# gMLP mixing on column halves of the array, a 768-byte gap between FFN operands, and an alternating unit order

## What is computed

```python
u, v = split(gelu(h @ w_in)); v = rms_norm(v, v_gain)           # both [T, 1024]
ws = where(chunk_causal_mask(128), w_s, 0.0)                    # 16 groups of [128, 128]
vb = v.reshape(B, nb, 128, 16, 64)                              # blocks of 128 rows, groups of 64 channels
mixed = einsum('gpq,bnqgd->bnpgd', ws, vb) + b_s                # mixing of rows inside a block, by group
out = (u * mixed) @ w_out
```

## Time and profile before

| | |
|---|---|
| median of 3 runs | 2557.38 us (2556.01 to 2557.67) |
| profiled execution, own time | 2556.86 us |
| its span, first to last instruction | 2555.1 us |
| TensorE (PE) busy | 2500.5 us, 98% of the span, 16343 matmuls |
| weight loads (PEld) busy | 2424.3 us, 95% |
| VectorE (DVE), ScalarE (ACT), GpSimd (POOL) busy | 1513.9, 890.7, 258.8 us |
| large products on `gx` / on `h` | 10368 / 3168 matmuls of 128x352 |
| mixing matmuls, L1867 | 288 instructions, 33.9 us busy |
| mean granted TensorE clock | 0.991 |

### The profile page before, as it was taken

The page is one execution under the profiler, slowest core; times in us unless marked ns, Lnnn a source line. Parts: engine busy times, 40 slices in busy tenths (PEclk is TensorE's granted clock), DMA queues, the critical chain, the costliest instruction groups (busy, mean ns, idle before and its releaser), DMA issues.

```text
span 2555.1 us, 42749 instructions
## 1 busy us (share of the span) xinstructions
PE 2500.5 (98%) x16343; PEld 2424.3 (95%) x16343; DVE 1513.9 (59%) x2833; ACT 890.7 (35%) x1663; POOL 258.8 (10%) x569
## 2 busy tenths in 40 slices
PE   7999999999999999999999999999999999999998
PEld 7888888889899999999999999999999999999998
DVE  4555555567766666666666524334666666666666
ACT  5444444445422222222234531234222333222223
POOL 0111111102100000000001420221000000000003
PEclk9999999999999999999999999999999999999999
DMA  5222222444111011111111210111111111110112
GB/s 145 69 59 59 59 59 59 138 117 141 50 50 49 33 44 38 42 40 49 49 49 34 68 33 17 51 50 50 34 50 49 49 49 49 49 49 33 38 45 78
DMA packets 136980, 145.29 MB, mean 57 GB/s; under 512 B 4940, under 2 KB 126452, under 8 KB 136884
## 3 DMA queue, kind: packets, MB, share of 16 engines
q1 hardware_dynamic: 121844, 118.82, 14.6%
q0 software_dynamic: 14384, 23.03, 3.4%
q10 hardware_dynamic: 656, 2.12, 0.2%
HBM read 125.97 MB, written 17.97 MB: 56 GB/s over the span
## 4 chain that ended last, share of the span: by engine, by line
PE 89%; DVE 5%; ACT 3%; POOL 2%; issue 1%; DMA 0%; ACTq 0%; DVEq 0%; POOLq 0%
PE psum L158 26%; PE psum L160 26%; PE psum L159 26%; PE psum L1003 2%; PE psum L1024 2%; PE psum L986 2%; POOL total L229 1%; PE psum L1867 1%; DVE gx_lo L217 1%; PE psum L901 0%; ACT conv_t L1545 0%; DVE w_lo L763 0%; DVE conv_t L1615 0%; DVE conv_t L1618 0%; ACT w_hi L759 0%
## 5 line engine op out<-in xcount | busy, mean ns | idle before, releaser
L158 PE MATMUL psum<-gx_hi,w_hi 128*128 128x352 f32 x3456 | 1131.2, 327 | 15.7 <-DVE gx_lo L217 6.7
L159 PE MATMUL psum<-gx_lo,w_hi 128*128 128x352 f32 x3456 | 1119.5, 324 | 0.0
L160 PE MATMUL psum<-gx_hi,w_lo 128*128 128x352 f32 x3456 | 1118.6, 324 | 0.0
L158 PEld LDWEIGHTS psum<-gx_hi,w_hi 128*128 128x128 f32 x3456 | 652.7, 189 | 20.7 <-issue 14.3
L159 PEld LDWEIGHTS psum<-gx_lo,w_hi 128*128 128x128 f32 x3456 | 653.2, 189 | 0.6 <-issue 0.5
L160 PEld LDWEIGHTS psum<-gx_hi,w_lo 128*128 128x128 f32 x3456 | 652.9, 189 | 0.0
L1642 DVE TENSOR_TENSOR x<-x,psum 128x352 f32<-128x352 f32 x528 | 259.3, 518 | 123.0 <-PE psum L160 123.0
L1545 ACT ACTIVATE conv_t<-a_gate,cur 128x352 f32<-128x352 f32 x132 | 90.1, 683 | 535.4 <-DVE a_gate L1605 535.3
L158 PE MATMUL psum<-h_hiA,w_hi 128*128 128x352 f32 x528 | 172.7, 327 | 9.8 <-issue 5.5
L158 PE MATMUL psum<-h_hiB,w_hi 128*128 128x352 f32 x528 | 172.8, 327 | 0.0
L160 PE MATMUL psum<-h_hiB,w_lo 128*128 128x352 f32 x528 | 172.4, 326 | 0.0
(11 more groups left out here) (189 smaller groups left out, 2898.7 us busy)
## 6 DMA issues: line engine op xcount, KB each, us to landing
raw<-in_f_w_up SPq DMA_DIRECT2D x44, 1024.0 KB, 5.0
raw<-in_f_w_down SPq DMA_DIRECT2D x22, 1024.0 KB, 4.7
raw<-in_a_w_o SPq DMA_DIRECT2D x25, 512.0 KB, 3.9
raw<-in_a_w_qkv SPq DMA_DIRECT2D x24, 512.0 KB, 3.8
raw<-in_b_w_in SPq DMA_DIRECT2D x8, 1024.0 KB, 5.6
raw<-in_b_w_out SPq DMA_DIRECT2D x4, 1024.0 KB, 5.2
gx_hi<-o_scratch POOLq DMA_DIRECT2D x3, 1232.0 KB, 6.3
gx_lo<-o_scratch POOLq DMA_DIRECT2D x3, 1232.0 KB, 9.9
```

What stands on the lines that cost most here:

```text
L158: pe.matmul(out, w[0], rhs[0], start=first, stop=False)
L159: pe.matmul(out, w[0], rhs[1], start=False, stop=False)
L160: return pe.matmul(out, w[1], rhs[0], start=False, stop=last)
```

## The change

The mixing writes the first group of a pair to PSUM partitions 0 to 63 and the second to 64 to 127 (`HEAD_ROWS`), each by a matmul of its own with 64 stationary columns. The zero columns go, and with them `v_pad`, two memsets of POOL and VectorE's split into halves; `v_n` holds the plain block. `mix_done` is raised by both last matmuls. One DMA stores the sample rows' `v` in place of two. A gap of 192 float32 (768 bytes) is put between `h_hiB` and `h_loA`, so the distance from high to low half is 9216 bytes. In the down stage the outputs with odd `d` take unit B first.

```diff
-        ("h_hiA", [P, TW], F32R), ("h_hiB", [P, TW], F32R), ("h_loA", [P, TW], F32R), ("h_loB", [P, TW], F32R),
+        ("h_hiA", [P, TW], F32R), ("h_hiB", [P, TW], F32R), ("h_gap", [P, -2 * TW % 256], F32), ("h_loA", [P, TW], F32R), ("h_loB", [P, TW], F32R),
...
-    vT, vt0, vt1, wsT, bs, gain_v, gm_t, rc_v = region(
-        ("vT", [P, KT, TW], F32), ("vt0", [P, KT, 2, P], F32), ("vt1", [P, KT, 2, P], F32),
+    vT, ws_raw, v_n, wsT, bs, gain_v, gm_t, rc_v = region(
+        ("vT", [P, KT, TW], F32), ("ws_raw", [P, GROUPS, P], F32), ("v_n", [P, 2, D], F32),
...
-                    for i in range(2):
+                    turn = (0, 1) if d % 2 == 0 else (1, 0)
+                    for i in turn:
                         mm = product(pe, psum[:, n % ring, :CH[c][1]], (f_hi[2 + i][:, cut], f_lo[2 + i][:, cut]),
-                                     (chunk(h_hi[i][:, :], c), chunk(h_lo[i][:, :], c)), i == 0, i == 1)
+                                     (chunk(h_hi[i][:, :], c), chunk(h_lo[i][:, :], c)), i == turn[0], i == turn[1])
...
             if b == 0:
-                pe.wait_ge(g_zero, 3)
+                pe.wait_ge(g_zero, 1)
...
-                for h in range(2):
-                    mm = pe.matmul(psum[:, 4 + 2 * (b % 2) + d // 4, P * (d % 4):P * (d % 4) + n],
-                                   v_pad[b % 2][:n, d, h, :], wsT[:n, 2 * d + h, :n], start=(h == 0), stop=(h == 1))
-            mm.then_inc(mix_done, 1)
+                for h, half in enumerate(HEAD_ROWS):
+                    mm = pe.matmul(psum[half, 4 + 2 * (b % 2) + d // 4, P * (d % 4):P * (d % 4) + n],
+                                   v_n[:n, b % 2, P * d + HALF * h:P * d + HALF * (h + 1)], wsT[:n, 2 * d + h, :n],
+                                   start=True, stop=True)
+                    if d == KT - 1:
+                        mm.then_inc(mix_done, 1)
...
             for bank in range(2):
-                src = psum[:n, 2 * (b % 2) + bank, :].rearrange("p (k h e) -> p k h e", h=2, e=HALF)
-                g = gain_v[:n, :].rearrange("p (k h e) -> p k h e", h=2, e=HALF)[:, 4 * bank:4 * bank + 4]
-                for h in range(2):
-                    mm = dve.scalar_tensor_tensor(v_pad[b % 2][:n, 4 * bank:4 * bank + 4, h, HALF * h:HALF * (h + 1)],
-                                                  src[:, :, h, :], rc_v[:n, b:b + 1], g[:, :, h, :], ALU.mult, ALU.mult)
+                cut = slice(BANK * bank, BANK * (bank + 1))
+                mm = dve.scalar_tensor_tensor(v_n[:n, b % 2, cut], psum[:n, 2 * (b % 2) + bank, :], rc_v[:n, b:b + 1],
+                                              gain_v[:n, cut], ALU.mult, ALU.mult)
...
-        pool.wait_ge(ws_in, 16)
-        pool.memset(vt1[:, :, :, :], 0.0).then_inc(g_zero, 1)
         with pool.Fori(1, SETS) as i:
             sums(i, False)
+        pool.wait_ge(v_added, NCH * KT)
         pool.wait_ge(ws_copied, GROUPS // 4)
-        pool.memset(vt0[:, :, :, :], 0.0).then_inc(g_zero, 1)
-
-        pool.wait_ge(g_zero, 2)
         pool.memset(wsT[CK:, :, :CK], 0.0).then_inc(g_zero, 1)
```

More of the change, by code:

```diff
@@ L115, in build @@
     probs = [(pA0, pB0), (pA1, pB1)]
-    (raw1, w_hi2, w_hi3, w_lo2, w_lo3, a_gate, a_val, s_gate, h_hiA, h_hiB, h_loA, h_loB,
+    (raw1, w_hi2, w_hi3, w_lo2, w_lo3, a_gate, a_val, s_gate, h_hiA, h_hiB, h_gap, h_loA, h_loB,
      conv_t, prod, cur, tails, tails_row) = region(
@@ L1763, in g_sp @@
         region_free(sp)
-        sp.dma_start(vt0[:, :, :, :].rearrange("p k h n -> p (k h) n"), b_w_s[0].rearrange("g p q -> p g q"))\
+        sp.dma_start(ws_raw[:, :, :], b_w_s[0].rearrange("g p q -> p g q"))\
             .then_inc(ws_in, 16)
@@ L1839, in g_pe @@
                 g = 4 * j + k
[L1840 removed]
+                mm = pe.transpose(psum[:, 6 + j % 2, P * k:P * (k + 1)], ws_raw[:, g, :], ident[:, :])
             mm.then_inc(ws_turned, 1)
@@ L1998, in turn @@
             dve.wait_ge(vt_turned, b + 1)
-            at_least(dve, mix_done, b - 1)
+            at_least(dve, mix_done, 2 * (b - 1))
             for bank in range(2):
-                src = psum[:n, 2 * (b % 2) + bank, :].rearrange("p (k h e) -> p k h e", h=2, e=HALF)
-                g = gain_v[:n, :].rearrange("p (k h e) -> p k h e", h=2, e=HALF)[:, 4 * bank:4 * bank + 4]
-                for h in range(2):
-                    mm = dve.scalar_tensor_tensor(v_pad[b % 2][:n, 4 * bank:4 * bank + 4, h, HALF * h:HALF * (h + 1)],
-                                                  src[:, :, h, :], rc_v[:n, b:b + 1], g[:, :, h, :], ALU.mult, ALU.mult)
+                cut = slice(BANK * bank, BANK * (bank + 1))
+                mm = dve.scalar_tensor_tensor(v_n[:n, b % 2, cut], psum[:n, 2 * (b % 2) + bank, :], rc_v[:n, b:b + 1],
+                                              gain_v[:n, cut], ALU.mult, ALU.mult)
             mm.then_inc(vt_copied, 1)
@@ L2009, in mix @@
             start, n = BLOCKS[b]
-            dve.wait_ge(mix_done, b + 1)
+            dve.wait_ge(mix_done, 2 * (b + 1))
             for bank in range(2):
@@ L2245, in gmlp_over @@
         engine.wait_ge(gs_lo, NCH * KT)
-        engine.wait_ge(gv_out, 32)
+        engine.wait_ge(gv_out, 16)
     ffn = []
@@ L2270, in _ @@
         final_sp(sp)
-        for semaphore, stores in ((k_out, 2 * PAIRS), (v_out, 2 * PAIRS), (gv_out, 2), (Ffn.tails_out, 2 * DEPTH),
+        for semaphore, stores in ((k_out, 2 * PAIRS), (v_out, 2 * PAIRS), (gv_out, 1), (Ffn.tails_out, 2 * DEPTH),
                                   (y_out[0], 3), (y_out[1], 3), (y_out[2], 3)):
```

8 lines of the change are left out of this document (2 added, 6 removed).

## The result

The changed kernel took 2538.68 us, the median of four runs (2535.27, 2536.72, 2540.65, 2541.03); the kernel before, in four runs beside them, 2557.26. The ratio is 0.9928, 95% interval 0.9916 to 0.9939: 18.6 us or 0.7% less, clear of the scatter of both. The forecast was 2536.1, in a range of 2531 to 2545.

A forecast was written before the change was run, and what follows sets the result against it. The prediction took TensorE, busy in 98% of the span, to bound the kernel. From 2556.86 us it took 15.3 for the mixing and 6.0 for the down stage, giving 2535.6, as median 2536.1; range 2531 to 2545.

The forecast's parts named there:

- before mix(0): Start of the mixing: VectorE's copy of block 0 goes from 1.66 to 1.28 us, 0.4 us gained.
- six periods: Mixing from mix(0) to mix(6): the period falls from 4.45 to 2.87 us, 9.5 us gained.
- mix(6) and the end: Last blocks of the mixing: mix(6) itself gains 1.7 us, the end where VectorE becomes the bound 3.75 us.
- clock behind the mixing: Matmuls after the mixing at low clock: their 2.0 us loss kept unchanged, with 2 us either way in the range.
- down stage: FFN down stage: gap and new order gain 6.0 us, bounds 0 to 6.9.
- Passes on halves: Mixing: 32 passes at 0.0547 us take 1.75 us in place of 3.57; array changes cost 0.235 us a period.
- VectorE's copy: Mixing: two operations of 512 elements take 1.28 us, bounds 1.2 to 1.66, leaving TensorE the bound.
- T: End of mix(6), 1557.82 before; copy(8) starts at T + 0.28, mix(8) at T + 3.0, TensorE resumes at T + 5.0.
- that rival: Clock falls to 0.50 during the mixing, half the stationary columns being in use; time 2551 us, chance 0.06.
- The gap and the halves' distance: Down stage: high-to-low distance of 9216 bytes, 9 times 1024, removes the 2.3 ns excess per matmul; 6.0 us gained.
- the gap does nothing: Rival, down stage: the 2.3 ns belong to the bank change or output waits; time 2542.1 us, chance 0.17.
- Slower by the new order: Rival, down stage: new order makes it worse; 2566.5 us at 170 ns for all matmuls, chance 0.03.

The follow-up runs named there:

- e4: The changed kernel without the gap, alternating unit order kept; 2535.52 us, one run.
- e2: The kernel before with only the new down stage (gap and alternating unit order), old mixing kept; 2554.71 us, ratio 0.999 to before.
- m1: Against e4, VectorE's copy of a block in four operations of 256 elements again; 2535.53 us, one run.
- x2: Against the new mixing with the old down stage, unit A's weights loaded for both units (timing only); iteration 69.447 us.
- x4: Against the new mixing with the old down stage, 256 bytes put between the units' weight buffers; iteration 69.447 us.
- e3: The changed kernel with the gap but fixed unit order, A always first; 2544.06 us, one run, iteration 69.447 us.
- x1: Against the new mixing with the old down stage, unit A's activations read for both units (timing only); iteration 69.300 us.
- y1: Against x1, all four activation buffers moved 128 bytes further (timing only); 2539.73 us, one run, iteration 69.380 us.
- y2: Against e4, each activation chunk in 384 columns, so every start lies 128 bytes off a multiple of 256; 2533.75 us, one run.
- x3: Against the new mixing with the old down stage, 384 bytes put between the units' activation buffers; iteration 69.407 us.

## Why the prediction was right, and where it failed

The direction and the range held; the time was 2.6 us too low. The range could not have told the down stage's part from nothing, since 2542.1, the time without it, lies inside too; so each term is held against its own stretch:

| term | forecast, us | measured, us | from |
|---|---|---|---|
| before mix(0) | 0.4 | -1.5 (this execution), -0.2 (e4) | table of stretches; e4 |
| six periods | 9.5 | 6 x (4.45 - 2.92) = 9.2 | after |
| mix(6) and the end | 1.7 + 3.75 | 14.60 - 9.2 = 5.4 | after |
| clock behind the mixing | 0 | 1.0 (e4 2.3; e2, with the old mixing, 1.3) | stretch to the first down stage of layer 1 |
| down stage | 6.0 | 22 x 0.14 = 3.1 | after, e2, e4 |

- **Passes on halves.** Right: 32 passes and both array changes in a period took 2.92 - 0.88 = 2.04 us; 32 x 0.0547 leave 0.29 for the changes. Forecast 0.235. The two distances that it counted came out as forecast: last transpose to first pass 0.20 us, 0.09 above the usual, and last pass to first transpose 0.20 us, 0.15 above the mean of a pass. It left out the distance behind, from the first transpose to the second, 0.16 us for 0.11. That 0.055 is the whole difference between 2.87 and 2.92. The attention in the kernel before has it too, in the transpose behind the one at 304.24 of the earlier trace rows:

```profile
304.41 0.27 PE L1003 MATMUL psum<-ident,pB 128*128 128x128 f32 x1
```

  The 0.0547 came out right with some luck: by single starts, the 19 distances of the earlier trace rows are ten of 7 ns inside a pair and nine between pairs, where a steady stream has as many of the one as of the other, and the first of the nine is 0.05 us longer, behind the change of width. The two cancel. The rule of the Trainium skill (page "TensorEngine Tiling (Array Packing)", section "Key Properties"), that a change of tiling mode drains the array, was weighed at 0.43 us a period; the trace gives 0.29, nearer to the attention's rows than to a wait for a full matmul at each change.
- **VectorE's copy.** Forecast 1.28 for two operations of 512, measured 1.41. It cost nothing in the periods, as m1 shows, and stood in the bounds (1.2 to 1.66).
- **The end.** T is 1548.05 by the same reading (copy(8) starts 0.27 us after it at 1548.32), mix(8) starts at T + 3.0 as forecast, and TensorE resumes at T + 5.1, forecast T + 5.0. mix(8) took 1.12 us for 0.9.
- **The clock.** Full in the mixing's periods, so that rival is out. Behind it the low level lasted for 10 matmuls in place of 16, where I had set no gain. It isn't shown that the change made it: e2, with the old mixing, has as short a way from the next product to the down stage (247.4 us) as the changed kernel (247.7), and in x2 and x4, with the new one, the first matmuls behind the mixing run at 160 ns from the start. At the start it fell earlier in this execution than in that of before, and e2 did the same with the old mixing. The forecast gain of 0.4 us there can't be read from one execution, and m1 against e4 (0.25 us for the copy) doesn't settle it.
- **The gap and the halves' distance: this step failed.** The prediction said of the distance from high to low half, modulo 1024 bytes, that it "is the one thing that the two stages differ in and that the gap makes equal", and built 6.0 us on it. (They differ in the PSUM bank's turns too, as the next paragraph of the prediction says itself.) e3 has the gap and nothing of the gain. The gain is that of the order, 3.1 us, to which the prediction gave no gain of its own. It takes 0.14 of an excess of 0.32 us an iteration that depends on where the moving operands start, not on the distance between two: x1 against y1 and y2 show it. My rival "the gap does nothing" was right on the gap; its number, 2542.1, held nothing from the order, while the measured 2538.7 lies between the two cases.
- **Slower by the new order.** Out: every kind of step was as good or better.
- **The rule that places don't matter.** The Trainium skill, page "SBUF — State Buffer", section "SBUF: two separate sides", says that within the engine side "only the shared port pair causes contention". It speaks of engines that wait for one another and not of addresses; that neither gap nor order could act was my reading of it. x1 against y1 is the same program 128 bytes further, and its excess changes chunks, so the measurement decides against this reading.

What stays open. The experiments show that the place of the moving operands sets the excess, and a layout without it; they don't give the rule. Counting only matmuls that start on a multiple of 256 bytes, at 19 ns for six: before has 3 of 6 in each output, so 9.5 ns, and shows 17, 12 and 12; the alternating order has the same starts in runs of six instead of three and shows 8, 7 and 8; x3 has 2, 4 and 2 of 6, so 6.3, 12.7 and 6.3, and shows 9, 13 and 10. The count is roughly right for x3 and leaves out something that depends on the order, which no run isolates. Nor does the excess sit where the count puts it. In the trace of before, from the third output of a chunk on, B's three matmuls take 13 ns over 480 and A's 7 in chunk 0, where B is aligned; but in chunk 1, where A is aligned, A's take nothing over and B's 13, and in chunk 2, where B is, B's take nothing and A's 13. So either the time is lost some matmuls late, or the step between an aligned and an unaligned operand has a part in it. And y1's chunk 0 has 13 ns where six aligned starts gave 18 and 19 elsewhere. All starts tried lie on a multiple of 256 or 128 bytes off one; other remainders weren't tried. And the up stage has such starts too (`gx_hi` starts at byte 50304, 196.5 x 256, and its tiles are 16.5 x 256 bytes apart, so every second one is aligned) and costs nothing, 160.0 ns a matmul. What differs there is not known; the PSUM bank, which changes every 24 matmuls there and every 6 in the down stage, is one candidate, and what the other engines read and write meanwhile another; neither was tried.

## What to carry to other kernels

When two groups fill only half of the stationary columns each, give each its own column half instead of padding with zeros: the two halves then work side by side and a pass costs half, while changing the array's width and back took 0.29 us, so by these numbers it pays from about six passes on (0.29 / 0.057, an estimate). A mean distance between starts that is 1% above that of equal work elsewhere is worth an experiment on addresses before a theory: change one operand to the same buffer, and see which chunks lose their excess. And judge a change of a few microseconds by the stretch that it touches; the whole time of one and the same kernel scattered by more than the down stage gave.

## What the hardware showed that was not expected

- The start address of a moving operand can matter to TensorE: in the down stage 128x352 matmuls took 160.0 ns when all starts lay 128 bytes off a multiple of 256 (y2), and 162.2 (y1, chunk 0) to 163.2 ns (x1, chunk 1) when all lay on one; a shift of the buffers by 128 bytes moved the excess from one chunk to the other two. In the up stage, with starts of both kinds, it didn't matter.
- The place of the stationary operand didn't matter (69.447 us in x2 and x4 against 69.447).
- Two passes on different column halves start 7 ns apart, and each pair takes the 0.109 us of one transpose at full width.
- Two executions with the same mixing and the same down stages (after and e4) differed by 5.5 us, nearly all of it in the stretches where TensorE waits or its granted clock falls.
